# Strassen's seven products for 18 blocks of a projection, feature-major queries and keys, and eight weight blocks moved out of attention

## The reference

```python
h = x @ w_in[i]
ua, va, za, qh, kh, vh, zb, ga, gb = jnp.split(h, IN_OFFSETS, axis=-1)
ua = jax.nn.gelu(ua, approximate=False)
...
q = apply_rope(qh.reshape(bn, s_len, B_HEADS, 2, B_QK_DIM), cos, sin) * (B_QK_DIM ** -0.5)
k = apply_rope(kh.reshape(bn, s_len, B_HEADS, 2, B_QK_DIM), cos, sin)
...
o = diff_attention(q, k, vh.reshape(bn, s_len, B_HEADS, B_V_DIM), lam)
o = rms_norm_2(o, b_subln_g[i]) * (1.0 - lam_init)
yb = o.reshape(bn, s_len, B_WIDTH) * jax.nn.silu(zb)
merged = jax.nn.sigmoid(ga) * (ya @ w_branch_a[i]) + jax.nn.sigmoid(gb) * (yb @ w_branch_b[i])
```

## Time and profile before

| | us |
|---|---|
| median of 3 runs | 2541.99 |
| lowest and highest | 2539.81, 2542.74 |
| span of the profiled execution (its own time isn't shown apart) | 2544.3 |
| PE busy | 2425.4 (95%) |
| PE weight loads busy | 2128.2 (84%) |
| DVE busy | 1172.9 (46%) |
| ACT busy | 908.8 (36%) |
| POOL busy | 748.5 (29%) |
| second projection, by the timeline | 1100 to 1465 |
| attention, by the timeline | 1465 to 2209 |

### The profile page before, as it was taken

One profiled execution on the slowest core, in us unless ns is written; L12 is line 12 of the kernel. 1 busy time (PEld: TensorE's weight loads), 2 busy tenths in 40 slices (PEclk: granted clock), 3 DMA queues, 4 the chain that ended last, 5 costly groups with the idle time before them and its releaser, 6 DMA issues.

```text
span 2544.3 us, 41785 instructions
## 1 busy us (share of the span) xinstructions
PE 2425.4 (95%) x16392; PEld 2128.2 (84%) x16392; DVE 1172.9 (46%) x2536; ACT 908.8 (36%) x1686; POOL 748.5 (29%) x725
## 2 busy tenths in 40 slices
PE   6999989999998798999999999999999999999996
PEld 5778968888787698999999889777899777787795
DVE  3001349999996333140000053454454464577535
ACT  4214554444443233131121233333333343554321
POOL 3112224545543121222213232332332332232123
PEclk9999999999999899999999999999999999999998
DMA  4323343343333422132223233133233225375611
GB/s 184 125 108 133 117 158 133 121 142 112 113 132 124 164 103 99 66 115 96 79 95 112 82 117 108 50 124 112 70 105 108 90 89 187 118 270 193 217 54 67
DMA packets 155118, 305.01 MB, mean 120 GB/s; under 512 B 11456, under 2 KB 79680, under 8 KB 143696
## 3 DMA queue, kind: packets, MB, share of 16 engines
q1 hardware_dynamic: 90704, 214.73, 24.2%
q10 hardware_dynamic: 64256, 88.10, 9.7%
HBM read 203.69 MB, written 99.09 MB: 119 GB/s over the span
## 4 chain that ended last, share of the span: by engine, by line
PE 71%; issue 14%; DVE 8%; DMA 2%; POOL 2%; ACT 2%; POOLq 0%; SPq 0%; DVEq 0%; ACTq 0%
PE bank L393 11%; PE bank L395 10%; PE bank L394 10%; PE bank L404 8%; PE bank L405 7%; PE bank L406 7%; PE bank L2087 3%; PE bank L2067 3%; POOL w_lo L359 1%; PE bank L1384 1%; PE bank L2056 1%; PE bank L676 1%; PE bank L2371 1%; DVE w_lo L359 1%; DVE rec_z L1119 1%
## 5 line engine op out<-in xcount | busy, mean ns | idle before, releaser
L404 PE MATMUL bank<-w_hi,at_hi 128*128 128x256 f32 x2432 | 705.7, 290 | 7.7 <-DVE at_lo L1584 6.8
L405 PE MATMUL bank<-w_lo,at_hi 128*128 128x256 f32 x2432 | 692.6, 285 | 0.0
L406 PE MATMUL bank<-w_hi,at_lo 128*128 128x256 f32 x2432 | 692.5, 285 | 0.0
L393 PE MATMUL bank<-at_hi,w_hi 128*128 128x512 f32 x1472 | 608.8, 414 | 5.9 <-ACT stage L429 5.5
L395 PE MATMUL bank<-at_hi,w_lo 128*128 128x512 f32 x1472 | 578.8, 393 | 0.0
L394 PE MATMUL bank<-at_lo,w_hi 128*128 128x512 f32 x1472 | 577.4, 392 | 0.0
L359 POOL TENSOR_TENSOR w_lo<-w_raw,w_hi 128x2048 fp32r<-128x2048 f32 x69 | 318.2, 4611 | 843.3 <-ACT w_hi L372 843.3
L404 PEld LDWEIGHTS bank<-w_hi,at_hi 128*128 128x128 f32 x2432 | 471.7, 194 | 20.9 <-issue 12.0
L405 PEld LDWEIGHTS bank<-w_lo,at_hi 128*128 128x128 f32 x2432 | 471.0, 194 | 0.8 <-issue 0.2
L406 PEld LDWEIGHTS bank<-w_hi,at_lo 128*128 128x128 f32 x2432 | 470.5, 193 | 0.0
L429 ACT ACTIVATE stage<-bank 128x512 f32<-128x512 f32 x272 | 161.9, 595 | 623.4 <-PE bank L395 320.0
(11 more groups left out here) (256 smaller groups left out, 2958.3 us busy)
## 6 DMA issues: line engine op xcount, KB each, us to landing
w_raw<-in_weights SPq DMA_DIRECT2D x84, 1024.0 KB, 7.0
feat<-stage ACTq DMA_DIRECT2D x152, 256.0 KB, 2.0
tok<-stage ACTq DMA_DIRECT2D x104, 256.0 KB, 2.2
stage<-feat SPq DMA_DIRECT2D x32, 256.0 KB, 3.5
x<-in_x SPq DMA_DIRECT2D x4, 1024.0 KB, 9.6
w_mem<-in_w_mem SPq DMA_DIRECT2D x4, 1024.0 KB, 11.5
logg<-gate_g ACTq DMA_DIRECT2D x8, 512.0 KB, 2.8
rec_b<-logg SPq DMA_DIRECT2D x16, 256.0 KB, 5.2
```

What stands on the lines that cost most here:

```text
L393: nc.tensor.matmul(ps_gemm[i % 2], wh, ah, start=(k == 0), stop=False)
L404: nc.tensor.matmul(o, ah, wh, start=(k == 0), stop=False)
L405: nc.tensor.matmul(o, ah, wl, start=False, stop=False)
L406: last = nc.tensor.matmul(o, al, wh, start=False, stop=(k == KT - 1))
```

## The change

- Queries, keys, ZB, UA and the first half of ZA, 18 blocks, are computed in `p5_*` by Strassen's scheme (in the form with seven products and shared sums). A block is cut into 2 x 2 quarters: weights by features (two halves of 512) and by columns (two of 128), activations by features and by tokens (two of 512). Seven products of a quarter by a quarter, each 4 k x 3 matmuls of 512 columns, replace eight.
- The four differences of the activations, t1 to t4, and their high and low parts are made once (`quarter_differences`, twelve DVE operations of 128x2048 and four ACT copies of the same size). The sums of weight quarters are made for each block by DVE (`weight_sums`), the host laying the weights out by quarters. ACT makes the high parts of three sums (wx_hi, 128x1536) beside w_hi, POOL the low parts.
- The products alternate between the two PSUM banks. ACT copies the first product out and one corner, DVE adds up the three other corners from PSUM and SBUF into stage, and ACT stores them (with silu in place for ZB).
- Queries and keys lie feature-major in feat2. For each head SP loads them as [128, 1024], and in a second buffer with the halves of 32 rows swapped (five DMAs each). The rotation is three operations of [128, 1024], with tables of [128, 1024] made after the Strassen blocks. The 16 transposes of a head and the copies da_qT and da_kT are gone; the rotated tiles are the operands of the scores, in two buffers for heads in turn.
- The other half of ZA, two blocks, follows the 18 in form F. Attention keeps 16 blocks, two to a head, 32 parts; the first scores of a head are issued before the last slot of the head ahead.

```diff
-UA, ZA, ZB, GA, GB = 0, 1024, 2048, 3072, 4096
-ROWS2 = GB + D
-VA, QH, KH, VH, PG = 0, D, 2 * D, 3 * D, 4 * D
+UA, ZA, ZB, GA, GB, QF, KF = (n * D for n in range(7))
...
-            Segment(8, "T", ACT.Copy, tok2, QH),
-            Segment(4, "T", ACT.Copy, tok2, VH),
+        gemm2 = [Segment(4, "T", ACT.Copy, tok2, VH)]
+        gemm_quarters = [
+            Segment(4, "F", ACT.Copy, feat2, QF),
+            Segment(4, "F", ACT.Copy, feat2, KF),
             Segment(4, "F", ACT.Silu, feat2, ZB),
+            Segment(4, "F", ACT.Copy, feat2, UA),
+            Segment(2, "F", ACT.Copy, feat2, ZA),
         ]
+        gemm_before = [Segment(2, "F", ACT.Copy, feat2, ZA + 2 * CB)]
         def load_pair(sp, pair):
...
-        SLOT_PARTS = [5] + [2, 0, 2] * LONG + [3, 1, 2] * LONG + [3]
+        SLOT_PARTS = [2] + [2, 0, 1] * LONG + [2, 1, 1] * LONG + [2]
...
-            Segment(4, "F", ACT.Copy, feat2, UA),
-            Segment(4, "F", ACT.Copy, feat2, ZA),
...
+        def quarter_product(pe, bank, left, right, start):
+            (wh, wl), (ah, al) = left, right
+            for k in range(QUARTER):
+                c = slice(k * P, (k + 1) * P)
+                nc.tensor.matmul(bank, wh[:, c], ah[:, k, :], start=(start and k == 0), stop=False, skip_group_check=True)
+                nc.tensor.matmul(bank, wh[:, c], al[:, k, :], start=False, stop=False, skip_group_check=True)
+                last = nc.tensor.matmul(bank, wl[:, c], ah[:, k, :], start=False, stop=(k == QUARTER - 1), skip_group_check=True)
+            return last
...
+        def quarter_block(pe, m):
+            g, b = Q_AT + m, m % 2
+            even, odd = ps_gemm[b], ps_gemm[1 - b]
+            l11, l12, l22, s3 = [(loaded_part(w_hi, b, n), loaded_part(w_lo, b, n)) for n in range(4)]
+            s1, s2, s4 = [(wx_hi[b][:, n, :], wx_lo[b][:, n, :]) for n in range(3)]
+            r11, r21, r22 = [(quarter(at_hi, *at), quarter(at_lo, *at)) for at in ((0, 0), (1, 0), (1, 1))]
+            t1, t2, t3, t4 = (t1_hi, t1_lo), (t2_hi, t2_lo), (t3_hi, t3_lo), (t4_hi, t4_lo)
+            pe.wait_ge(w_split, g + 3)
+            if m:
+                pe.wait_ge(q_dve, 5 * m + 1)
+            else:
+                pe.wait_ge(tile_out, 4 * g + 1)
+            quarter_product(pe, even, l11, r11, True).then_inc(q_done, 1)
+            if m:
+                pe.wait_ge(q_dve, 5 * m + 2)
+            else:
+                pe.wait_ge(tile_out, 4 * g + 2)
+                pe.wait_ge(fill_lo, FILLED3 - 1)
+            quarter_product(pe, odd, s2, t2, True).then_inc(q_done, 1)
+            pe.wait_ge(q_act, 2 * m + 1)
+            quarter_product(pe, even, l12, r21, False).then_inc(q_done, 1)
+            pe.wait_ge(q_dve, 5 * m + 3)
+            quarter_product(pe, odd, s3, t3, True).then_inc(q_done, 1)
+            pe.wait_ge(q_act, 2 * m + 2)
+            quarter_product(pe, even, s1, t1, True).then_inc(q_done, 1)
+            pe.wait_ge(q_dve, 5 * m + 4)
+            if m == 0:
+                pe.wait_ge(fill_lo, FILLED3)
+            quarter_product(pe, odd, l22, t4, False).then_inc(q_done, 1)
+            pe.wait_ge(q_dve, 5 * m + 5)
+            last = quarter_product(pe, even, s4, r22, False)
+            if m < Q_N - 1:
+                last.then_inc(q_done, 1)
+            else:
+                last.then_inc(tile_done, 4 * Q_N)
...
+        def weight_sums(dve, m):
+            b = m % 2
+            raw = [raw_part(b, n) for n in range(4)]
+            dve.wait_ge(w_loaded[b], ((Q_AT + m) // 2 + 1) * 16)
+            if m:
+                dve.wait_ge(w_split, Q_AT + m + 2)
+            link(dve, nc.vector.tensor_tensor(xs[:, 0, :], raw[3], raw[2], ALU.add))
+            nc.vector.tensor_tensor(raw[3], raw[0], raw[3], ALU.subtract)
+            link(dve, nc.vector.tensor_tensor(xs[:, 1, :], xs[:, 0, :], raw[0], ALU.subtract))
+            nc.vector.tensor_tensor(xs[:, 2, :], raw[1], xs[:, 1, :], ALU.subtract).then_inc(q_sums, 1)
...
+        def weight_lows(pool, m):
+            b, g = m % 2, Q_AT + m
+            pool.wait_ge(w_high, g + 1)
+            pool.tensor_tensor(wx_lo[b][:], xs[:], wx_hi[b][:].bitcast(F32), ALU.subtract)
+            split_low(pool, g // 2, b)
...
+        def quarter_results(act, m):
+            b, func = m % 2, Q_BLOCKS[m][0].func
+            if m < Q_N - 1:
+                sums_high(act, m + 1)
+            act.wait_ge(q_done, PRODUCTS * m + 1)
+            if m >= 2:
+                block_sums_done(act, m - 2)
+            nc.scalar.activation(xu[:, b, :], ps_gemm[b], ACT.Copy).then_inc(q_act, 1)
+            if m < Q_N - 1:
+                loaded_high(act, m + 1)
+            else:
+                high_before(act, 0)
+            act.wait_ge(q_done, PRODUCTS * m + 3)
+            corner_free(act, m, 0)
+            nc.scalar.activation(stage[:, 0, :], ps_gemm[b], func).then_inc(q_act, 1)
+            act.wait_ge(q_act, 2 * m + 2)
+            store_corner(act, m, 0)
+            act.wait_ge(q_dve, 5 * m + 5)
+            store_corner(act, m, 3)
+            act.wait_ge(q_dve, 5 * m + 6)
+            store_corner(act, m, 2)
+            block_sums_done(act, m)
+            store_corner(act, m, 1)
...
+        def quarter_sums(dve, m):
+            b = m % 2
+            even, odd = ps_gemm[b], ps_gemm[1 - b]
+            u = xu[:, b, :]
+            dve.wait_ge(q_done, PRODUCTS * m + 2)
+            dve.wait_ge(q_act, 2 * m + 1)
+            nc.vector.tensor_tensor(u, odd, u, ALU.add).then_inc(q_dve, 1)
+            dve.wait_ge(q_done, PRODUCTS * m + 4)
+            dve.wait_ge(q_dve, 5 * m + 3)
+            corner_free(dve, m, 3)
+            nc.vector.tensor_tensor(stage[:, 3, :], odd, u, ALU.add).then_inc(q_dve, 1)
+            dve.wait_ge(q_done, PRODUCTS * m + 5)
+            dve.wait_ge(q_dve, 5 * m + 4)
+            nc.vector.tensor_tensor(stage[:, 3, :], even, stage[:, 3, :], ALU.add).then_inc(q_dve, 1)
+            if m + 2 < Q_N:
+                weight_sums(dve, m + 2)
+            dve.wait_ge(q_done, PRODUCTS * m + 6)
+            corner_free(dve, m, 2)
+            nc.vector.tensor_tensor(stage[:, 2, :], odd, u, ALU.add).then_inc(q_dve, 1)
+            block_products_done(dve, m)
+            corner_free(dve, m, 1)
+            last = nc.vector.tensor_tensor(stage[:, 1, :], even, u, ALU.add)
+            if m < Q_N - 1:
+                last.then_inc(q_dve, 1)
+            else:
+                last.then_inc(tile_out, 4 * Q_N)
...
+            for b in range(2):
+                for i in range(4):
+                    whole_tile(pe, s, 1, b, i)
+            for m in range(Q_N):
+                quarter_block(pe, m)
+            gemm_pe(pe, gemm_before)
...
+            for segs in (gemm2, gemm_quarters):
+                gemm_sp(sp, segs)
+            sp.wait_ge(tile_done, ALL_QUARTERS + 8)
...
+            row = head * P
+            if head >= 2:
+                sp.wait_ge(d_s, (head - 1) * 16 + 1)
+            if head:
+                sp.wait_ge(d_rq, 3 * head)
+                sp.wait_ge(d_rk, 3 * head)
+            for x, swapped, at, done in ((dqx[head % 2], dqs, QF + row, d_in), (dkx[head % 2], dks, KF + row, d_in)):
+                sp.dma_start(x[:], feat2[at:at + P, :]).then_inc(done, 16)
+                for n in range(4):
...
+                eng.wait_ge(ready, 160 * (head + 1))
+                eng.tensor_tensor(to[:], to[:], dcos[:], ALU.mult).then_inc(done, 1)
             elif third == 1:
-                eng.tensor_tensor(tmp[:, 2], x2, c, ALU.mult).then_inc(done, 1)
-                eng.tensor_tensor(tmp[:, 3], x1, s, ALU.mult).then_inc(done, 1)
+                eng.tensor_tensor(swapped[:], swapped[:], dsin[:], ALU.mult).then_inc(done, 1)
             else:
...
-            dve.wait_ge(d_tk, it + 1)
-            nc.vector.tensor_copy(dkT[:], ps_b[:].rearrange("p a n -> p (a n)")).then_inc(d_ek, 1)
...
-            act.wait_ge(d_tq, it + 1)
-            nc.scalar.activation(dqT[:], ps_a[:].rearrange("p a n -> p (a n)"), ACT.Copy).then_inc(d_eq, 1)
+            attention_exp(act, it, 0)
             slot_results(act, it, FIRST_SLOT)
-            attention_exp(act, it, 0)
...
+            first_scores(pe, 0)
             for head in range(B_HEADS):
                 head_pe(pe, head)
+        def first_scores(pe, it):
+            pe.wait_ge(d_rq, 3 * it + 3)
+            pe.wait_ge(d_rk, 3 * it + 3)
+            pe.wait_ge(d_e, it * 16 + 2)
+            attention_scores(pe, it, 0)
...
-            pe.wait_ge(d_e, it * 16 + 2)
-            for x, ps, done, ready in ((dq, ps_a, d_tq, d_rq), (dk, ps_b, d_tk, d_rk)):
-                pe.wait_ge(ready, it * 6 + 6)
-                for t in range(NT):
-                    last = nc.tensor.transpose(ps[:, t // 4, (t % 4) * P:(t % 4 + 1) * P],
-                                               x[:, t].rearrange("p m a n -> p (m a n)"), ident[:])
-                last.then_inc(done, 1)
             slot_products(pe, it, FIRST_SLOT)
```

(5 more changed lines are left out.)

273 lines of the change are left out of this document (190 added, 83 removed).

## The result

The changed kernel is slower. Its median is 2578.93 us in four runs (2570.61 to 2580.82), against 2540.9 us for the kernel before beside it; the ratio is 1.0144, with a 95% interval of 1.0128 to 1.016, so 38 us more where I had forecast 42 us less. The profiled execution has a span of 2576.7 us, a time of 2578.53 and a mean clock of 0.965 (before: 2544.3 and 0.981).

The account below looks back on a forecast made before the run. TensorE's instruction stream was taken to bound the kernel. Terms -72.5 + 2.9 + 1.8 + 23.2 + 2.5 = -42.1 took 2541.99 us to about 2500; forecast 2487 to 2515 (0.67), range 2476 to 2527.

Parts of the forecast that it names:

- The PE work, -72.5: Queries, keys, silu gates, UA and half of ZA by seven products, and transposes gone: 72.5 us less TensorE time.
- The Strassen stage's waits, 0: In the 18 Strassen blocks other engines keep up with one microsecond spare: 0, bound 3.6 us a block.
- the missed microsecond: Rival, 0.06: in Strassen blocks POOL ends too late, each block waits for its fourth corner; 18 to 65 us more.
- the seams: Rival: each of 126 Strassen products has a 0.26 us seam, 33 us more; chance included in the missed microsecond's 0.06.
- DVE held by POOL: Rival, 0.12: in attention POOL's w_lo, twice a head, falls on DVE's rotation or da_a; 29 to 64 us more.
- ACT's order: In attention's turn 4, w_hi runs ahead of the da_aT copy on ACT, so PE waits 1.9 us per head.
- The other five tile ends: Tiles ending ahead of transposes in attention turns 0, 3, 5, 6, 7: 0.38 us each, 1.9 per head.
- +23.2: Attention's waits for ACT: 3.8 us a head times 8, 30.4, less 7.2 already there; bounds 0 and 61.
- The handoff, +2.9: At attention's start PE has less cover and waits 4.4 us for the first da_a, against some 1.5 before.
- The last head, +2.5: In attention's last head DVE waits for the gelu on ACT, then does statistics, with a shorter turn; 0 to 5.
- The clock, +1.8: A clock drop behind the wait at attention's start, costed at 1% of 184 us.
- Slower than before: Rival, 0.03: attention loses the cover that hid its chain; gain gone at 9.1 us waits a head, about 2625 us.

Follow-up runs that it names:

- ten blocks with early loads: Changed kernel with UA and ZA back in attention, only ten blocks by seven products, and v and gate loaded a head early: 2495.47 us.
- the early loads: Changed kernel with v and gate in two buffers each, loaded by SP one head ahead: 2519.33 us, ratio 0.9925 to the kernel before.
- the runs with ten blocks: Changed kernel with UA and ZA back in attention: 2522.42 us; with v and gate a head early 2495.47; with two further repairs 2489.62.

## Why the prediction was wrong

- **The PE work, -72.5: right.** Strassen blocks are 19.04 us, as forecast; queries, keys, ZB and transposes bring what they should (ten blocks with early loads, 44 of 50.7).
- **The Strassen stage's waits, 0: right,** but for one of 0.9 us at its end. 341.07 of 342 us busy. The rivals of the missed microsecond and of the seams are out.
- **The loads: the step that failed.** It stood nowhere in the sum, and so was costed at nothing. I wrote of the rotation tables, of DVE's wider rotations and of when the queries would be read, but not that "queries, keys and rotation feature-major" puts eight more loads, 1 MB, on the same DMA engines in the 4 us in which v and gate of the head are issued. Nor did I ask what held SP back: the waits for da_qT and da_kT, which go with the transposes, had kept its loads 2.2 to 3.5 us behind v. The trace of before had v and gate at 5.9 and 7.1 us to landing, with two loads of 512 KB a head behind them; in the changed kernel the output product stands 8.0 us behind gate's issue. A rise of one microsecond had to show, and it rose by 7.5. That is 46.2 us of waits (38.8 beside the queries' loads, 7.4 in the last head beside loads of the old size that start sooner), and some 18 of the 29 us of clock, as with the early loads 21.0 us of busy time in place of 57.5 are left at half the clock. For the first seven heads the swapped rows' bytes are shown as the cause by their removal; for the last head the early issue is read off the two traces, and no run moved it alone.
- **DVE held by POOL (rival, 0.12): its mechanism came true, at a place I had excluded.** I said that POOL does w_lo behind its root, when da_a is done. For the last slot it does so at the start of the next head, ahead of da_a of turn 0, and the held operation was one of 128 x 1. Price 21.3 - 7.8 = 13.5 us, below my 29 to 64, and none of it visible while the loads were late. Once it also came as I had described it, on da_a itself, in the last head, beside POOL's w_lo of 2205.10 to 2209.79; PE then waits 1.87 us:

```profile
2205.39 5.21 DVE L2154 SCALAR_TENSOR_TENSOR da_a<-da_p,small 128x768 f32<-128x768 f32 x1
```

- **ACT's order, 1.9 us a head at turn 4: right, at 1.7 in seven of the eight heads.** The other five tile ends I took at 0.38 each; on PE they cost 0.2 us once. So +23.2 was 12.2. The 0.38 came from waits of the weight loads, which rose from 4.6 to 18.4 us, and a weight load that waits does not always hold a matmul.
- **The handoff, +2.9: about right in its own wait,** 3.45 us against the 4.4 forecast, but 3.50 us more followed, for v and gate of head 0 (PE's timeline):

```profile
1583.18 0.48 PE L2320 MATMUL bank<-ident,da_a 128*128 128x128 f32 x1 [3.45 <-DVE da_a L2154]
...
1589.71 0.65 PE L2331 MATMUL bank<-da_v,da_aT 128*128 128x128 f32 x2 [3.50 <-issue]
```

- **The last head, +2.5: right.** DVE idles 4.32 us for the gelu and then has its 2.68 us of statistics, and PE waits 2.52 us for da_a. The 2.5 us for at_lo just behind attention I had not looked for.
- **The clock, +1.8: wrong by a factor of 16,** because it follows the waits.
- **"Slower than before" (0.03)** was the side that came true, with 9.1 us of waits per head as its point; 80.3 / 8 = 10.0 were there. But its mechanism, an engine's own chain without cover, was at most half of it. The lost cover is in the waits for da_a and da_aT and in half of those at the output product, as the runs with ten blocks show; what stood uncovered was a group of loads first of all, and a single wait on SP's queue takes 54 us away. The range, 2476 to 2527, holds the repaired versions, not the change. It was also narrower than I said: with my own upper bound of 61 us for attention's waits the sum gives 2538.

## What to carry to other kernels

When a change alters how data is laid out, list its DMAs first: which loads are issued in the same microseconds, in how many bytes, and who waits for the last of them; a load that was on time by one microsecond is a bound in waiting. Ask also which wait kept a load back: when the work that it waited for goes, the load starts sooner, beside others. A transfer needed soon goes ahead of one that has a whole head's time, by one wait or by a second buffer. And when a wait is removed and the time stands still, look whether it went into the next one: two repairs that bring 60 and 2 us alone brought 80 together.

## What the runs showed of the hardware

- **A DVE operation of 128 x 1 elements with two SBUF operands took 3.07 us, at most 3.46, beside a POOL subtraction of 4.57 us,** and 0.16 in the median. It ended when POOL's did (1660.22 + 3.07 and 1658.70 + 4.57, both 1663.3), so it is POOL's remaining time that counts, not the size of what is held. With POOL's subtraction moved it took 159 to 161 ns in all 64 cases. (The Trainium skill, GPSIMD Engine Reference, Specifications, names contention for such instructions; the runs agree, and put it at some 20 times the duration of a small one.)
- **1 MB of loads in bands of 32 partitions delayed two others by 4.2 and 6.3 us** in the median, while all engines were busy at 241 to 332 GB/s, where 310 to 410 were moved without them.
- **The same loads, issued with v and gate instead of 3.5 us behind v, made these land 14.7 and 16.8 us after issue in place of 5.9 and 6.0** (the last head, the changed kernel and the one before).
- **A float32 matmul of the identity with itself, 128 columns, took 0.227 us (44 in 9.98), a transpose of the same size 0.10 us** (sixteen in the 1.66 us of the earlier trace rows; the 0.13 that I went by is eight in 1.04, which overlap the next eight), at the full clock.
- **The half clock costs half of the busy time in it, not of its length:** of 85.3 us at 0.50, 57.5 were busy, so 29 us and not 43. PE's busy time bears it out: it fell by 44.6 us, where 72.5 us of work went.
